# TensorE's order of work within a step of mixer B and of the hybrid layers: the projection unit first, the attention work second

## The chip, the cores and the metric

The kernel runs on one core of one Trainium2 chip. The metric is the device time of one execution in microseconds (us); the number reported is the median of the runs. Lower is better.

## What is computed

A stack of four layers on 256 tokens of width 2048, all in float32: layer A (full attention with rotary positions), a gated convolution FFN, layer B (sliding windows with three dilations), the same FFN again, and two "hybrid" layers, each with four kinds of attention side by side.

```python
h = h + mixer_a(rms_norm(h), ...)          # 16 heads
h = h + conv_ffn(rms_norm(h), ...)
h = h + mixer_b(rms_norm(h), ...)          # 24 heads of 128, three groups with dilation 1, 4, 16
h = h + conv_ffn(rms_norm(h), ...)
x = rms_norm(h, final_norm)
for l in range(2):                         # hybrid_layer
    p = split_columns(rms_norm_2(x) @ w_in + b_in)
    # stick-breaking, native sparse, forgetting and latent attention, 4 heads each, each times silu(gate)
    x = x + rms_norm_2(mix @ w_out, post_g)
```

## The kernel before

**Weights come in units.** Every weight matrix is cut into units of at most 128 x 2048 numbers (1 MB), numbered through the whole kernel. Unit u is loaded by a DMA on SyncE's queue (`load_unit`, line 218), five ahead. For full accuracy each number is split into a high part, made by ScalarE (`split_high`, line 234), and a low part, made by VectorE (`split_low`, line 242). TensorE multiplies high by high, high by low and low by high (lines 259 to 261 for products with tokens in the columns, lines 270 and 280 for products with channels in the columns). When TensorE has finished a unit it raises `w_used`, and buffers come free by that count.

**Mixer B and the hybrid layers are pipelines of steps.** Each engine has its own program: a loop over steps s, with one unit for each step (96 steps in mixer B, 82 in a hybrid layer). The first steps project the input with `w_qkv` or `w_in` (`pe_project`; 72 steps in mixer B, O0 = 66 in a hybrid layer), the last ones multiply the attention's output by the output weights (`pe_out`). The attention of a head is spread over the steps by a fixed plan: `heads_at(s, lag)` in mixer B, and `score_at`, `turn_at`, `value_at` of each `Head` in the hybrid layers. `pe_heads` does TensorE's share: values of one head, transposes of another, scores of a third. `pe_jobs` and `pe_compress` do small products and transposes that prepare keys and values, and `pe_roots` one in mixer B.

Below, U(s) is the unit of step s on TensorE and H(s) all attention work of step s (heads, jobs, compress, roots). Before, TensorE's order is ... U(s-1), H(s), U(s), H(s+1) ...

**The other engines' programs**, which the change leaves as they are, run in this order in step s of a hybrid layer (mixer B is alike):

- VectorE (`vector`): normalise the weights of the last head (`dve_weights`); evict the product of the item (a group of 2 or 4 units) that ended with U(s-1) (`dve_evict`, lines 2686 and 2690, or 2681); multiply a head's output by its gate (2766); take the scores that H(s) made (2713); low part of a head's output (2775); side work (`dve_other`); at last `split_low` of unit s+2.
- ScalarE (`scalar`): copy half of the product out of PSUM (`act_halves`, 2517); `split_high` of unit s+2; jobs; place the evicted product, with SiLU for a gate (`act_place`, 2526); copy the turned weights (2580), exponentials (2588, and 2593 to 2599 for the stick-breaking heads, the logarithm being 2596); high part of a head's output (2603).

Each of these engines does its list strictly in order, so a wait inside step s holds back what stands behind it.

**What TensorE waits for ahead of a unit**: for the high or the low part of the unit's weights; at the first unit of an item for the eviction of the item two back (`taken`; the products alternate between two pairs of PSUM banks, 4/5 and 6/7); and `pe_out` in its first step (j == 0, step O0 = 66) for the eviction of all items, the last of which ended with U(65).

In the hybrid layers units differ in length: items of type "tok" have 4 units of 258 to 512 columns, and the narrow ones are short. Steps 6 to 13, 18 to 25 and 46 to 53 have short units of about 3 us, the others take 5.5 to 5.8 us.

Of the kernel before, what the change touches and what calls it, by code (L numbers as in the profile page):

```python
# [1632 lines left out]
class MixerB:  # L1633
# [118 lines left out]
    def tensor(self, pe):  # L1752
        for s in range(B_STEPS + 24):
            self.enter.enter_pe(pe, s)
            self.pe_roots(pe, s)
            self.pe_heads(pe, s)
            if s < B_STEPS:
                self.pe_project(pe, s)
            else:
                self.pe_out(pe, s)  # L1760

    def pe_roots(self, pe, s):

        c = self.c
        if s == 5:
            self.enter.await_row(pe)
            for b in range(TB):
                ins = pe.matmul(c.bank[1][:, b:b + 1], c.row[0:1, b::2], c.ident[0:1, 0:1], start=True, stop=True)
            ins.then_inc(self.roots_made, 1)

    def pe_project(self, pe, s):
        c = self.c
        m, q = b_unit(s)
        g, kind = m % 9 // 3, m % 3
        u = self.u0 + s
        if q == 0 and m >= 2:
            pe.wait_ge(self.taken, m - 1)
        if m == 0:
            self.enter.await_chunks(pe, 8 * q + 7)
        first = 4 + 2 * (m % 2)  # L1780
        if kind < 2:
            wide_high(c, pe, u, c.psum[:, first:first + 2, :], 8 * q)
            wide_low(c, pe, u, c.psum[:, first:first + 2, :], 8 * q).then_inc(c.w_used, 1)
            return
        pe.wait_ge(c.w_low, u + 1)
        wh, wl = split_view(c, u)
        for i in range(2):
            tokens = slice(i * P, (i + 1) * P) if g == 0 else slice(i, S, 2)
            for k in range(8):
                kt = 8 * q + k  # L1790
                ins = three(pe, c.bank[first + i][:, 0:S], c.hh[:, kt, tokens], c.hl[:, kt, tokens], wh[:, k, :], wl[:, k, :],
                            kt == 0, kt == KT - 1)
        ins.then_inc(c.w_used, 1)
# [252 lines left out]
class Hybrid:  # L2046
# [235 lines left out]
    def tensor(self, pe):  # L2282
        c = self.c
        for s in range(O0 + KT):
            self.enter.enter_pe(pe, s)
            self.pe_heads(pe, s)
            self.pe_jobs(pe, s)
            self.pe_compress(pe, s)
            if s < O0:
                self.pe_project(pe, s)  # L2290
            else:
                self.pe_out(pe, s - O0)

    def pe_project(self, pe, s):
        c = self.c
# [745 lines left out]
```

## Time and profile before

| | us |
|---|---|
| median of 3 runs (3349.14 to 3351.03) | 3349.6 |
| the profiled execution | 3350.5 |
| its span, first to last instruction | 3348.7 |
| TensorE busy in that span | 3290.2 |
| VectorE busy | 2020.5 |
| ScalarE busy | 1630.5 |
| mixer B | about 1035 to 1613 in the span |
| first hybrid layer | about 2355 to 2846 |
| second hybrid layer | about 2846 to 3335 |

The span is a single execution; all rows below are of it. Times in the rows count from the start of the span. "Idle before" in square brackets is the time that the engine stood still just before the row, and the arrow tells what ended it. TensorE's matmuls are pipelined: one starts before the last has ended, so the distance between starts is the cost of one, not its printed duration.

### The profile page before, as it was taken

The numbers are of one execution on the slowest core, as the hardware profiler recorded it, in microseconds if no ns is written. First come the engines' busy times: TensorE is split into PE (matmuls) and PEld (weight loads), VectorE is DVE, ScalarE is ACT, GpSimd is POOL, SyncE is SP. The second block draws the span as 40 slices with busy tenths as digits, with TensorE's granted clock in tenths as the row PEclk, the third lists the DMA queues.
The fourth block names the chain that finished last, engine by engine and source line by source line (L and its number), as shares of the span: only waits on it lengthen the run. The fifth ranks groups of instructions, "written<-read, shape, count | busy, mean of one in ns | idle before, by whom it ended". The sixth has DMA issues, their size and how long they took to land. (4 is left out here: it accounts for less than half of the span.)

```text
span 3348.7 us, 43197 instructions
## 1 busy us (share of the span) xinstructions
PE 3290.2 (98%) x18176; PEld 2855.8 (85%) x18176; DVE 2020.5 (60%) x2448; ACT 1630.5 (49%) x1875; POOL 0.2 (0%) x4
## 2 busy tenths in 40 slices
PE   8999999999999999999999999999999999999998
PEld 7768888888888999998888888888898987898986
DVE  6765774774665555555666576576565654664654
ACT  5554553553444444443554355354454753464743
POOL 0000000000000000000000000000000000000000
PEclk9999999999999999999999999999999999999999
DMA  6525556556556555555555555555754446754544
GB/s 224 179 79 187 189 195 208 190 192 221 189 201 195 182 183 180 185 179 180 183 189 194 198 189 189 194 188 183 227 174 142 154 155 229 224 170 138 164 155 176
DMA packets 498937, 615.54 MB, mean 184 GB/s; under 512 B 21733, under 2 KB 383359, under 8 KB 497720
## 3 DMA queue, kind: packets, MB, share of 16 engines
q1 hardware_dynamic: 495288, 606.49, 54.7%
q10 hardware_dynamic: 3456, 6.29, 0.6%
q8 instruction: 144, 2.36, 0.3%
q14 instruction: 49, 0.40, 0.1%
HBM read 606.39 MB, written 12.63 MB: 185 GB/s over the span
## 5 line engine op out<-in xcount | busy, mean ns | idle before, releaser
L242 DVE TENSOR_TENSOR low<-raw,high 128x2048 fp32r<-128x2048 f32 (+3 forms) x564 | 1243.3, 2205 | 900.2 <-ACT high L234 895.5
L234 ACT ACTIVATE high<-raw 128x2048 fp32r<-128x2048 f32 (+3 forms) x564 | 1042.4, 1849 | 1259.2 <-PE bank L280 612.0
L270 PE MATMUL bank<-h,high 128*128 128x512 f32 x4672 | 1124.4, 393 | 3.0 <-PEq L1656 1.0
L270 PEld LDWEIGHTS bank<-h,high 128*128 128x128 f32 x4672 | 859.9, 188 | 178.1 <-issue 9.2
L280 PEld LDWEIGHTS bank<-h,low 128*128 128x128 f32 x4672 | 599.0, 191 | 22.7
L280 PE MATMUL bank<-h,low 128*128 128x256 f32 x4672 | 606.0, 283 | 0.0
L259 PE MATMUL bank<-high,y_high 128*128 128x512 f32 x1208 | 473.6, 392 | 4.0 <-DVE hy_tmp L2686 2.3
L261 PE MATMUL bank<-high,y_low 128*128 128x512 f32 x1208 | 471.5, 390 | 0.0
L260 PE MATMUL bank<-low,y_high 128*128 128x512 f32 x1208 | 471.4, 390 | 0.0
L259 PE MATMUL bank<-high,h 128*128 128x256 f32 (+4 forms) x1112 | 362.0, 326 | 1.9 <-PEq L1032 1.0
L261 PE MATMUL bank<-high,h 128*128 128x256 f32 (+4 forms) x1112 | 354.1, 318 | 0.0
L260 PE MATMUL bank<-low,h 128*128 128x256 f32 (+4 forms) x1112 | 353.8, 318 | 0.0
L259 PEld LDWEIGHTS bank<-high,y_high 128*128 128x128 f32 x1208 | 227.7, 188 | 51.4 <-DVE hy_tmp L2686 2.8
L261 PEld LDWEIGHTS bank<-high,y_low 128*128 128x128 f32 x1208 | 227.5, 188 | 47.8
L260 PEld LDWEIGHTS bank<-low,y_high 128*128 128x128 f32 x1208 | 227.7, 188 | 46.3
L259 PEld LDWEIGHTS bank<-high,h 128*128 128x128 f32 x1112 | 212.9, 191 | 16.8 <-issue 1.8
L260 PEld LDWEIGHTS bank<-low,h 128*128 128x128 f32 x1112 | 212.9, 191 | 13.6
L261 PEld LDWEIGHTS bank<-high,h 128*128 128x128 f32 x1112 | 212.4, 191 | 14.1
L1161 DVE SCALAR_TENSOR_TENSOR st_cv<-st_v,conv,st_cv 128x255 f32<-128x255 f32 x352 | 142.7, 480 | 0.0
L1087 ACT ACTIVATE st_cv<-st_v,conv 128x256 f32<-128x256 f32 x176 | 91.2, 591 | 4.9 <-DVE st_v L1151 4.9
L2517 ACT ACTIVATE hy_tmp<-bank 128x512 f32<-128x512 f32 x34 | 20.3, 598 | 114.7 <-PE bank L280 114.7
L2686 DVE TENSOR_TENSOR hy_tmp<-bank,hy_tmp 128x512 f32<-128x512 f32 x34 | 23.5, 692 | 80.9 <-ACT hy_tmp L2517 80.9
(263 smaller groups left out, 1884.5 us busy)
## 6 DMA issues: line engine op xcount, KB each, us to landing
raw<-in_w_up SPq DMA_DIRECT2D x176, 1024.0 KB, 5.0
raw<-in_w_down SPq DMA_DIRECT2D x88, 1024.0 KB, 5.1
raw<-in_w_in SPq DMA_DIRECT2D x84, 1024.0 KB, 5.0
raw<-in_b_w_qkv SPq DMA_DIRECT2D x72, 1024.0 KB, 4.9
raw<-in_w_out SPq DMA_DIRECT2D x32, 1024.0 KB, 5.0
raw<-in_a_w_qkv SPq DMA_DIRECT2D x24, 1024.0 KB, 5.0
raw<-in_b_w_o SPq DMA_DIRECT2D x24, 1024.0 KB, 5.0
raw<-in_a_w_o SPq DMA_DIRECT2D x16, 1024.0 KB, 5.0
```

What stands on the lines that cost most here:

```text
L234: act.activation(c.high[u % SPLIT][:, 0:n], c.raw[u % RAW][:, 0:n], ACT.Copy).then_inc(c.w_high, 1)
L242: dve.tensor_tensor(c.low[u % RAW][:, 0:n], c.raw[u % RAW][:, 0:n], c.high[u % SPLIT][:, 0:n].bitcast(F32), ALU.subtract).then_inc(c.w_low, 1)
L259: pe.matmul(out, lh, rh, start=start, stop=False, skip_group_check=skip)
L260: pe.matmul(out, lh, rl, start=False, stop=False, skip_group_check=skip)
L261: return pe.matmul(out, ll, rh, start=False, stop=stop, skip_group_check=skip)
L270: pe.matmul(banks[:, i, :], wh[:, k, i * P:(i + 1) * P], c.h[:, k0 + k, :, :].rearrange("p a n -> p (a n)"), start=k0 + k == 0, stop=False ...
L280: ins = pe.matmul(banks[:, i, 0:S], wl[:, k, i * P:(i + 1) * P], c.hh[:, k0 + k, :], start=False, stop=k0 + k == KT - 1, skip_group_check= ...
L1087: act.activation(cv[:, par, q, :], v[:, par, q, :], ACT.Identity, bias=taps[:, 3, ch:ch + 1], scale=taps[:, 1, ch:ch + 1]).then_inc(centre ...
L1161: ins = dve.scalar_tensor_tensor(out=out, in0=v[:, par, q, src], scalar=taps[:, tap, ch:ch + 1], in1=out, op0=ALU.mult, op1=ALU.add)
L2517: act.activation(self.tmp[:, n % 2, :, :], c.psum[:, bank:bank + 2, S:2 * S], ACT.Copy).then_inc(self.halved, 1)
L2686: dve.tensor_tensor(tmp, c.psum[:, bank:bank + 2, 0:S], tmp, ALU.add).then_inc(self.taken, 2)
```

## The change

In both loops the call that does the step's unit is moved ahead of the calls that do the attention work. TensorE's order becomes ... H(s-1), U(s), H(s), U(s+1) ... The boundary work of the first steps (`enter_pe`) stays at the head of the step, and the work of the other engines, their order and all semaphores stay as they are.

```diff
@@ MixerB.tensor
         for s in range(B_STEPS + 24):
             self.enter.enter_pe(pe, s)
-            self.pe_roots(pe, s)
-            self.pe_heads(pe, s)
             if s < B_STEPS:
                 self.pe_project(pe, s)
             else:
                 self.pe_out(pe, s)
+            self.pe_roots(pe, s)
+            self.pe_heads(pe, s)
@@ Hybrid.tensor
         for s in range(O0 + KT):
             self.enter.enter_pe(pe, s)
-            self.pe_heads(pe, s)
-            self.pe_jobs(pe, s)
-            self.pe_compress(pe, s)
             if s < O0:
                 self.pe_project(pe, s)
             else:
                 self.pe_out(pe, s - O0)
+            self.pe_heads(pe, s)
+            self.pe_jobs(pe, s)
+            self.pe_compress(pe, s)
```

## Rows read from the trace of the kernel before

**Rows 1.** The page, part 1: busy time, share of the span, instructions.
```profile
PE 3290.2 (98%) x18176; PEld 2855.8 (85%) x18176; DVE 2020.5 (60%) x2448; ACT 1630.5 (49%) x1875; POOL 0.2 (0%) x4
```
**Rows 2.** Waits of TensorE, whole span: us in total, times, longest.
```profile
PE bank L2419 <- ACT x L2538: 2.9, 1, 2.9
PE bank L259 <- DVE hy_tmp L2686: 2.3, 2, 1.2
...
PE bank L2372 <- ACT hy_prob_t L2580: 0.8, 2, 0.4
```
**Rows 3.** Waits of TensorE in mixer B (1036 to 1613), the whole answer.
```profile
PE bank L270 <- PEq L1032: 1.0, 1, 1.0
```
**Rows 4.** Timeline of TensorE: start, us, what; H(65), U(65), H(66), U(66).
```profile
2744.37 0.59 PE L2372 MATMUL bank<-hy_prob_t,hy_vb 128*128 128x256 f32 x2
...
2747.01 3.94 PE L270 MATMUL bank<-h,high 128*128 128x512 f32 x16
...
2752.69 0.49 PE L2356 MATMUL bank<-ident,hy_prob 128*128 128x128 f32 x3
2754.34 0.50 PE L259 MATMUL bank<-high,y_high 128*128 128x512 f32 x1 [1.15 <-DVE hy_tmp L2686]
```
**Rows 5.** Timeline of VectorE: low part of unit 67, weights, eviction in step 66.
```profile
2748.31 2.29 DVE L242 TENSOR_TENSOR low<-raw,high 128x2048 fp32r<-128x2048 f32 x1
...
2750.71 0.55 DVE L2750 TENSOR_SCALAR hy_prob<-hy_prob,hy_rec 128x128 f32<-128x128 f32 x2
2753.59 0.69 DVE L2686 TENSOR_TENSOR hy_tmp<-bank,hy_tmp 128x512 f32<-128x512 f32 x1 [2.33 <-ACT hy_tmp L2517]
```
**Rows 6.** Stretches: busy us (count) of PE, PEld, DVE, ACT, POOL; PEclk; DMA share; GB/s.
```profile
2376.20:2379.50 3.30, 3.30 (x9) 2.54 (x8) 2.29 (x1) 3.30 (x4) 0.00 (x0) 0.50 0.00 1
2338.60:2345.40 6.80, 5.06 (x16) 4.38 (x17) 2.89 (x5) 3.05 (x9) 0.00 (x0) 0.50 0.25 95
2847.20:2854.00 6.80, 3.50 (x16) 3.27 (x16) 4.02 (x10) 3.26 (x8) 0.00 (x0) 0.50 0.09 30
2752.00:2762.00 10.00, 8.85 (x47) 7.35 (x46) 4.42 (x5) 6.78 (x7) 0.00 (x0) 1.00 0.38 110
```
**Rows 7.** Timeline of TensorE: the first rows after three long waits.
```profile
2375.43 0.71 PE L535 MATMUL bank<-ident,token_stat 128*128 128x128 f32 x4 [2.19 <-ACT token_stat L520]
2340.34 0.90 PE L438 MATMUL bank<-ident,x 128*128 128x128 f32 x3 [4.36 <-DVE x L384]
2850.50 0.90 PE L438 MATMUL bank<-ident,x 128*128 128x128 f32 x3 [7.07 <-DVE x L404]
```
**Rows 8.** Timeline of TensorE: H(45), U(45), H(46), and H(49).
```profile
2639.81 0.49 PE L2356 MATMUL bank<-ident,hy_prob 128*128 128x128 f32 x3
...
2640.60 4.02 PE L270 MATMUL bank<-h,high 128*128 128x512 f32 x16
...
2646.38 0.59 PE L2372 MATMUL bank<-hy_prob_t,hy_va 128*128 128x256 f32 x2
...
2657.56 0.51 PE L2356 MATMUL bank<-ident,hy_prob 128*128 128x128 f32 x3
```
**Rows 9.** Timeline of ScalarE: copy of step 45, eviction copy and logarithm of step 46.
```profile
2641.04 0.47 ACT L2580 ACTIVATE hy_prob_t<-bank 128x384 f32<-128x384 f32 x1
...
2646.62 0.60 ACT L2517 ACTIVATE hy_tmp<-bank 128x512 f32<-128x512 f32 x1 [2.10 <-PE bank L280]
...
2651.71 0.53 ACT L2596 ACTIVATE hy_a<-hy_a 128x384 f32<-128x384 f32 x1
```
**Rows 10.** Timeline of VectorE: step 47, from the stick-breaking head to unit 49's low part.
```profile
2652.27 0.56 DVE L2725 SCALAR_TENSOR_TENSOR hy_a<-hy_prob,hy_a 128x384 f32<-128x384 f32 x1 [2.05 <-ACT hy_a L2596]
...
2655.77 1.23 DVE L242 TENSOR_TENSOR low<-raw,high 128x1032 fp32r<-128x1032 f32 x1
```
**Rows 11.** Timeline of VectorE and TensorE: low part of unit 11; H(11).
```profile
2412.70 1.25 DVE L242 TENSOR_TENSOR low<-raw,high 128x1048 fp32r<-128x1048 f32 x1 [4.81 <-ACT high L234]
...
2417.57 1.85 PE L2402 MATMUL bank<-conv,y 128*128 128x15 f32 x16
```

## The prediction

> **What bounds the kernel now.** Read the busy times first: TensorE is busy 98% of the span, VectorE 60%, ScalarE 49% [rows 1]. So TensorE's stream sets the time, and the change neither adds nor removes an instruction in it. It can pay only where TensorE stands still, and cost only where it makes it stand still. So read TensorE's waits next. Of 58 us idle (3348.7 - 3290.2) most lie at the start, the end and the boundaries between stages, which this change doesn't reach. Inside the two loops three kinds are in reach [rows 2]: one wait of 2.9 us for a ScalarE copy (L2538, step 7 of the first hybrid layer), two of 1.2 us at the first output unit (once for each hybrid layer) and two of 0.4 us for the turned weights of a head. Mixer B has no wait inside its loop at all, only 1.0 us on entering it [rows 3]. So at most about 6 us can be won. The question is what can be lost.
>
> **What the change moves.** Comparing the two orders, all H(s) move behind U(s) and nothing else changes. Among themselves the H(s) keep their distance, one unit apart. Three kinds of dependence follow.
> (a) From H to H by way of ScalarE or VectorE: same distance as before, no effect.
> (b) From a unit to attention work: one more unit of slack.
> (c) From attention work to a unit, because VectorE and ScalarE stand in their own step s waiting for H(s), with splits and evictions queued behind: one unit less. The scores (L2713) wait for H(s); behind them stand `dve_other`, the low part of unit s+2, and the eviction of step s+1. The exponentials wait for those scores; behind them stand ScalarE's eviction copy and `split_high` of step s+1.
> SyncE's loads wait for `w_used` of units alone; U(s) now ends earlier by the length of H(s), so loads start no later. Its side transfers that wait for attention work (the bias rows in mixer B, `mla_w_uq` behind `product`) are due three steps or more later; I cost them at nothing.
> For (c) the splits have two units of lead and now keep one, 5.5 to 5.8 us, or 3 us in the short steps. The only place with no lead is `pe_out` at step 66: it needs the eviction of the item that ended with U(65).
>
> **Step 66 of each hybrid layer.** Before, U(65) ends at 2752.69, three transposes (H(66)) run, TensorE waits 1.15, and U(66) starts at 2754.34: 1.65 us from unit to unit, and H(65) cost 2747.01 - 2744.37 = 2.64 earlier [rows 4]. After, H(65) comes between U(65) and U(66), and VectorE must do all of step 65 behind it before it can evict. That chain stands in the rows as it would run, counted from the start of H(65) at 2744.37: scores, low part of unit 67 (from 2748.31, 2.29 us), exponentials on ScalarE beside it, weights done at 2750.71 + 0.55 = 2751.26 [rows 5]. Before, the eviction's first half then waited for U(65) and its copy; after, U(65) is long done, and ScalarE's copy (0.6 us) follows its exponentials and fits beside the low part. So the addition takes 0.69 at once, and TensorE starts 0.06 behind it, as in the rows (2753.59 + 0.69 to 2754.34): 2752.04, which is 7.7 us from the start of H(65). H(66) now costs its own time later, 0.3. Net: 7.7 + 0.3 - 2.64 - 1.65 = 3.7 us. TensorE stands still for 7.7 - 2.64 = 5.0 us, where it was 1.15.
>
> **What a long wait does to the clock.** Around the 1.15 us wait the granted clock stayed full, 1.00, that is 2.4 GHz (2752 to 2762) [rows 6]. After waits of 2.19, 4.36 and 7.07 us [rows 7] stretches at 0.50 (1.2 GHz) follow, with 3.30, 5.06 and 3.50 us of TensorE work in them [rows 6]. Work at half clock takes twice its time, so half of it is lost: 1.65, 2.5 and 1.75 us. The wait of 5.0 lies between the last two; I take 2.1 (bounds 1.6 and 2.5). Step 66: 3.7 + 2.1 = 5.8 for each layer, 11.6 for both.
>
> **The short steps 46 to 53.** Here ScalarE is nearly full: table loads for SiLU, logarithm and exponential alternate. Before, its copy of step 45 (line 2580) starts at 2641.04 and the logarithm of step 46 ends at 2651.71 + 0.53 = 2652.24: 11.2 us, of which 2.10 were a wait for U(45), so 9.1 us of work [rows 9]. After, the transposes that the copy needs come behind U(45), whose length is 2646.38 - 2640.60 = 5.78; they end at 2639.81 + 5.78 + 0.49 = 2646.1 [rows 8], and the logarithm ends at 2655.2. VectorE's step 47 hangs on it: 2657.00 - 2652.27 = 4.7 us from there to the low part of unit 49 [rows 10], which is ready at 2659.9. TensorE would come to U(49) where H(49) started before, 2657.56 [rows 8]. A new wait of 2.3 us. In exchange ScalarE's copy no longer lags behind the turns, and the 0.4 us wait at L2372 goes. Net 1.9. The wait is nearest to the one of 2.19, so its clock loss is taken as 1.6 (bounds 0 and 1.65). Both layers: 2 x 3.5 = 7.0. At step 66 the same lag can't add up: steps 54 to 60 have almost no attention work.
>
> **Step 7 of the first hybrid layer.** The 2.9 us wait goes: the jobs of step 6 come 3 us later and ScalarE, late because of a transfer, is ready in time for those of step 7. The half clock that follows it goes too. What is late next is the weights: unit 11's low part ends at 2412.70 + 1.25 = 2413.95, behind a transfer already issued, whereas H(11) started at 2417.57 before [rows 11]; U(11) now stands at that place. So the gain is 3.6 us, not the 4 or so that the wait and its clock make up. Bounds 2.9 and 4.0.
>
> **Sum.** 11.6 + 7.0 - 3.6 = +15.0 us. Against the profiled execution: 3350.5 + 15.0 = 3365.5. That execution was 0.9 above the median, so 3364.6. Mixer B: 0, and below zero excluded, since there is no wait to remove.
>
> **Rivals.**
> (A) The clock holds through the new short wait. For: 2.3 us is hardly more than 2.19, and waits of 1.15 cost nothing. Against: the rows after 2.19. It gives 3.2 less, 3361.4.
> The Trainium skill, "TensorE: Matmul & The Clock Gate", section "Why this matters for your kernels", names a length of idle gaps between bursts of matmuls that should be avoided, and 2.3 us is under it; by that rule this rival would be right. The trace's 2.19 us wait, with half clock after it, speaks against.
> (B) The lag in the short steps is absorbed and there is no new wait. Then 2 x 0.4 are won and not 7.0 lost: 11.6 - 0.8 - 3.6 = +7.2, 3356.8. It needs ScalarE to be 2.3 us quicker than its own rows; against it.
> (C) One more place in each layer loses its lead (class c). The thinnest are the low parts at step 20, where ScalarE has a new table load for the second compressed product between exponentials, and in mixer B at step 77, behind the sums. Priced like the short steps, 2 x 3.5: 3371.6.
> (D) Not slower: the place is step 66, the mechanism that the eviction isn't held behind H(65). If the chain from H(65) to the addition took under 4.3 us (2.64 + 1.65) instead of 7.7, the step would cost nothing: +15.0 - 11.6 = +3.4, 3353.0, which is no measurable change; with (B) as well, 3345.2. Against it: VectorE works its list in order and the low part of unit 67 alone is 2.29 of the chain.
> That the change doesn't do what it says I give no chance: TensorE runs its matmuls in program order.
>
> **How the numbers follow.** Forecast 0.48, A 0.20, B 0.14, C 0.10, D 0.08. A measurement of this kernel can tell about 0.2% from no change, 6.7 us, so 3356.3 and 3342.9 are the bounds. Slower: the forecast, A, C and half of B, 0.85. Same: the rest of B and most of D, 0.12. Faster: 0.03. The range takes in A and B and just reaches C: with the clock terms and the gain at step 7 at their bounds the forecast alone spans about 3363 to 3366, B lowers it to 3356, C raises it to 3371. 3355.5 to 3371.5.
>
> **What would show each step.** In the profile after: TensorE's wait at L259 for L2686 should be 2 x 5.0 in place of 2 x 1.2, with the granted clock at 0.50 behind it; a new wait at L259 for the low part (L242) of about 2.3 in each hybrid layer, ahead of U(49); no wait at L2419 and none at L2372; none in mixer B. ScalarE's and VectorE's busy times stay the same. The forecast is wrong if VectorE's eviction at step 66 comes sooner than 7 us after H(65) begins, or if waits stand at places not named here.

## The result, and the profile after

| | before | after |
|---|---|---|
| median, us | 3349.14 (5 runs, 3348.02 to 3351.03) | 3363.55 (5 runs, 3362.2 to 3364.64) |
| span of the profiled execution, us | 3348.7 | 3360.4 |

The changed kernel is slower by 14.4 us: ratio 1.0042, 95% interval 1.0031 to 1.0053, which is 10 to 18 us. The forecast was 3364.6. The profiled pair differs by 11.7 us; the section on the forecast shows where the rest lies.

Page of after, part 1 (busy time, share of the span, instructions). Beside [rows 1] every busy time stays within 5 us and the counts are the same: TensorE does no more work, it stands still longer.

```profile
PE 3293.6 (98%) x18176; PEld 2858.4 (85%) x18176; DVE 2015.8 (60%) x2448; ACT 1625.9 (48%) x1875; POOL 0.2 (0%) x4
```

Waits of TensorE in after, whole span (us in total, times, longest). The lines for L259 answer [rows 2]: the two waits for L2686 are 4.8 where they were 1.2, two waits for a low part (L242) are new, and L2419 and L2372 no longer appear. The last line is a wait of four transposes on entering the first hybrid layer; it stood in the kernel before too (its first row is in [rows 7]) and serves below.

```profile
PE bank L259 <- DVE hy_tmp L2686: 9.7, 2, 4.8
...
PE bank L259 <- DVE low L242: 4.4, 2, 2.2
...
PE bank L535 <- ACT token_stat L520: 2.2, 1, 2.2
```

The same view of after for mixer B (1030 to 1613), the whole answer: as [rows 3], nothing inside the loop.

```profile
PE bank L270 <- PEq L1656: 1.0, 1, 1.0
PE bank L270 <- PEq L1032: 1.0, 1, 1.0
```

**Step 66 of the first hybrid layer.** Timeline of TensorE in after (start, us, what): the first row is the start of H(65), the second the last of its scores, the third U(66), the fourth U(67), to be laid beside [rows 4].

```profile
2745.91 0.59 PE L2372 MATMUL bank<-hy_prob_t,hy_vb 128*128 128x256 f32 x2
...
2747.92 0.69 PE L2389 MATMUL bank<-hy_ck,ident 4*128 4x256 f32 x2
2753.44 0.79 PE L259 MATMUL bank<-high,y_high 128*128 128x512 f32 x1 [4.83 <-DVE hy_tmp L2686]
...
2761.79 0.47 PE L259 MATMUL bank<-high,y_high 128*128 128x512 f32 x1
```

Timeline of VectorE in after: low part of unit 67, then the weights, then the addition that U(66) needs.

```profile
2749.85 2.28 DVE L242 TENSOR_TENSOR low<-raw,high 128x2048 fp32r<-128x2048 f32 x1
2752.05 0.16 DVE L2739 RECIPROCAL hy_rec<-hy_tot 128x2 f32<-128x2 f32 x1
2752.24 0.55 DVE L2750 TENSOR_SCALAR hy_prob<-hy_prob,hy_rec 128x128 f32<-128x128 f32 x2
2752.70 0.68 DVE L2686 TENSOR_TENSOR hy_tmp<-bank,hy_tmp 128x512 f32<-128x512 f32 x1
```

Timeline of ScalarE in after: the eviction copy, done 1.3 us ahead of that addition.

```profile
2750.84 0.57 ACT L2517 ACTIVATE hy_tmp<-bank 128x512 f32<-128x512 f32 x1
```

There is no idle time on VectorE in these four rows, and the bank has been complete since U(65). The addition waits for its turn in VectorE's list.

**The short steps of the first hybrid layer.** Timelines of after, ScalarE (copy of step 45, logarithm of step 46), VectorE (start of step 47, low part of unit 49) and TensorE (U(49)), beside [rows 8 to 10]:

```profile
2640.16 0.49 ACT L2580 ACTIVATE hy_prob_t<-bank 128x384 f32<-128x384 f32 x1 [2.83 <-PE bank L2356]
...
2648.58 0.53 ACT L2596 ACTIVATE hy_a<-hy_a 128x384 f32<-128x384 f32 x1
```

```profile
2649.14 0.56 DVE L2725 SCALAR_TENSOR_TENSOR hy_a<-hy_prob,hy_a 128x384 f32<-128x384 f32 x1 [2.05 <-ACT hy_a L2596]
...
2652.64 1.22 DVE L242 TENSOR_TENSOR low<-raw,high 128x1032 fp32r<-128x1032 f32 x1
```

```profile
2653.92 0.39 PE L259 MATMUL bank<-high,h 128*128 128x258 f32 x1 [2.20 <-DVE low L242]
```

From the copy to the end of the logarithm 8.95 us, from there to the end of the low part 4.75, and TensorE starts within 0.1 us of that end. ScalarE now waits 2.83 for the transposes, which come behind U(45).

**The clock.** Stretches of after (busy us and count of PE, PEld, DVE, ACT, POOL; PEclk; DMA share; GB/s). From within the wait of 4.83 the granted clock is 0.50 (1.2 GHz) for 6.83 us; behind the wait of 2.20 it is 1.00 (2.4 GHz); and on entering the second hybrid layer, from within the 7.1 us wait, which ends at 2852.47, it is 0.50 for 13.65 us.

```profile
2752.02:2758.85 6.83, 5.41 (x13) 4.25 (x14) 4.56 (x8) 3.38 (x4) 0.00 (x0) 0.50 0.01 2
2653.90:2657.30 3.40, 3.38 (x28) 3.38 (x29) 2.75 (x5) 3.37 (x5) 0.00 (x0) 1.00 0.01 2
2847.60:2861.25 13.65, 7.86 (x26) 6.59 (x27) 9.30 (x21) 8.28 (x16) 0.00 (x0) 0.50 0.17 58
```

In the kernel before the same length at the same boundary was at half clock for only half of it:

```profile
2847.17:2860.82 13.65, 9.38 (x42) 7.99 (x43) 10.84 (x21) 6.75 (x13) 0.00 (x0) 0.75 0.05 16
```

### The profile page after: what moved, and what is told of

It is laid out like the page before. It is cut to its first block and busy times, and to the rows that moved or that the text cites. A ratio compares the mean times of both kernels' runs of the same rounds, so it can differ in the third digit from the quotient of the medians.

```text
span 3360.4 us, 43197 instructions
## 1 busy us (share of the span) xinstructions
PE 3293.6 (98%) x18176; PEld 2858.4 (85%) x18176; DVE 2015.8 (60%) x2448; ACT 1625.9 (48%) x1875; POOL 0.2 (0%) x4
## 5 line engine op out<-in xcount | busy, mean ns | idle before, releaser
L242 DVE TENSOR_TENSOR low<-raw,high 128x2048 fp32r<-128x2048 f32 (+3 forms) x564 | 1241.6, 2203 | 811.8 <-ACT high L234 807.5
L259 PE MATMUL bank<-high,y_high 128*128 128x512 f32 x1208 | 475.2, 393 | 11.4 <-DVE hy_tmp L2686 9.7
L259 PE MATMUL bank<-high,h 128*128 128x256 f32 (+4 forms) x1112 | 362.6, 326 | 6.5 <-DVE low L242 4.4
L259 PEld LDWEIGHTS bank<-high,y_high 128*128 128x128 f32 x1208 | 228.5, 189 | 59.1 <-DVE hy_tmp L2686 10.5
L259 PEld LDWEIGHTS bank<-high,h 128*128 128x128 f32 x1112 | 212.8, 191 | 22.4 <-DVE low L242 5.2
L260 PEld LDWEIGHTS bank<-low,h 128*128 128x128 f32 x1112 | 213.0, 192 | 13.8
L2713 DVE CUSTOM_DVE_ANT_0 hy_prob<-bank,hy_causal 128x128 f32<-128x128 f32 x64 | 20.3, 355 | 93.0 <-PE bank L2389 93.0
L451 ACT ACTIVATE h<-bank,gain 128x256 fp32r<-128x256 f32 x96 | 37.6, 476 | 66.7 <-PE bank L438 66.3
```

Source lines behind the costliest of these rows:

```text
L242: dve.tensor_tensor(c.low[u % RAW][:, 0:n], c.raw[u % RAW][:, 0:n], c.high[u % SPLIT][:, 0:n].bitcast(F32), ALU.subtract).then_inc(c.w_low, 1)
L259: pe.matmul(out, lh, rh, start=start, stop=False, skip_group_check=skip)
L260: pe.matmul(out, lh, rl, start=False, stop=False, skip_group_check=skip)
L451: ins = act.activation(c.hh[:, kt, :], self.bank(g, k // 2)[:, k % 2 * S:(k % 2 + 1) * S], ACT.Copy, scale=c.gain[:, self.gain_col + kt:se ...
L2713: ins = dve.tensor_tensor_reduce(self.prob[:, b, at:at + nk], c.bank[0][:, at:at + nk], mask, 1.0, -3e38, ALU.add, ALU.max, self.top[:, b, ...
```

## Experiments

Theory: all of the loss lies in the hybrid layers, at two places in each (step 66, and the short steps 46 to 53), less a gain at step 7 of the first. The main rivals: part of the loss comes from elsewhere, mixer B among it; and at step 66 something other than the order on VectorE and ScalarE holds the eviction. In the diffs `unit_first` picks the new order for single steps. Differences are to the median of the kernel before in the same comparison.

### One loop at a time

`b_only` turns the order in mixer B alone, `hybrid_only` in the hybrid layers alone.

```diff
@@ b_only: MixerB.tensor
-            self.pe_roots(pe, s)
-            self.pe_heads(pe, s)
...
+            self.pe_roots(pe, s)
+            self.pe_heads(pe, s)
@@ hybrid_only: Hybrid.tensor
-            self.pe_heads(pe, s)
-            self.pe_jobs(pe, s)
-            self.pe_compress(pe, s)
...
+            self.pe_heads(pe, s)
+            self.pe_jobs(pe, s)
+            self.pe_compress(pe, s)
```

> The unit goes first in mixer B alone; the hybrid layers keep the old order. My account: mixer B has no wait to win, and its splits keep a unit of lead, so 0 us against the kernel before (within 1 us), no wait of TensorE inside mixer B. Rival (the small places of class c matter): a wait at U(77) behind the sums, 0.1 to 2 us, and the time up by as much.

> The unit goes first in both hybrid layers alone. My account: all of the change, 12 to 15 us slower than before: two waits of 4.8 us at step 66, two of 2.2 us ahead of U(49), the 2.9 us wait of step 7 gone. If mixer B had a hidden part in it, the difference would be smaller by that part. Whether half clock follows the 2.2 us waits is open: in the profile of the changed kernel it did not; the forecast said it would, 1.6 us each.

Measured: b_only 3349.4 against 3349.26, ratio 1.0000 (0.9991 to 1.0009). hybrid_only 3364.59, ratio 1.0045 (1.0031 to 1.0059). The whole change is in the hybrid layers, and in mixer B it costs nothing that can be measured, as the list of waits above says. The profiles say it more finely than the medians, which are good to about 3 us: from 230 to 2300 us, which takes in all of mixer B, TensorE loses less than 0.2 us against before in b_only and in after.

### Without the new order at step 66

`old_from_60`: the changed kernel, with the old order from step 60 of the hybrid layers on.

```diff
+            unit_first = s < 60
+            if not unit_first:
+                self.pe_heads(pe, s)
+                self.pe_jobs(pe, s)
+                self.pe_compress(pe, s)
...
-            self.pe_heads(pe, s)
...
+            if unit_first:
+                self.pe_heads(pe, s)
...
```

> The changed kernel with the old order from step 60 on in the hybrid layers (steps 54 to 60 have next to no attention work, so the switch costs nothing). My account: the chain from H(65) to the eviction is what step 66 waits for; with H(65) ahead of U(65) again the wait is back at 1.2 us and each layer wins 6 us: 11 to 12 us faster than the changed kernel, about 3351 to 3352, and full clock at step 66. Rival (ScalarE and VectorE carry their lag from the short steps to the end of the layer): the wait at step 66 stays at 3 us or more.

Measured: 3352.18 against 3349.26, ratio 1.0009 (1.0000 to 1.0018). Against +14.4 of the whole change, +2.9 is left, so step 66 costs 11.5 us in both layers together; against hybrid_only, which ran in the same comparison, it is 12.4. Waits of TensorE, 2600 to 2760, the whole answer: the wait at step 66 is 1.2 again, the one ahead of U(49) stays. (Line numbers of this kernel are 6 higher behind line 2292; L2692 is L2686.)

```profile
PE bank L259 <- DVE low L242: 2.2, 1, 2.2
PE bank L259 <- DVE hy_tmp L2692: 1.2, 1, 1.2
```

The stretch behind that same 2.2 us wait is at half clock here, unlike in after:

```profile
2655.14:2658.55 3.41, 3.11 (x14) 3.11 (x15) 2.80 (x5) 3.38 (x5) 0.00 (x0) 0.50 0.12 43
```

### Without the lag in the short steps

`old_at_45`: the changed kernel, with the old order in step 45 alone, so that ScalarE gets the transposes of that step before U(45).

```diff
+            unit_first = s != 45
...
```

> The changed kernel with the old order in step 45 alone (H(45) ahead of U(45); H(44) is empty, so nothing else moves). My account: the wait ahead of U(49) comes from ScalarE's copy of step 45, which stood behind U(45). It goes: no wait for the low part (L242) in either layer, 2 x 2.2 us less than the changed kernel, some 3359. Rival (VectorE or ScalarE are simply full in the short steps, whatever H(45) does): a wait of 1 us or more stays ahead of some unit from 47 to 53.

Measured: 3357.05 against 3349.26, ratio 1.0024 (1.0014 to 1.0033). +7.8 are left, so the short steps cost 6.6 us in both layers together (7.5 against hybrid_only). That is more than the two waits of 2.2 that I expected to win. Waits of TensorE, 2600 to 3240, the whole answer: no L242 and no L2372, while the long wait of step 66 stays.

```profile
PE bank L438 <- DVE x L404: 7.1, 1, 7.1
PE bank L259 <- DVE hy_tmp L2692: 4.8, 1, 4.8
PE bank L259 <- DVE h L462: 0.9, 1, 0.9
```

One call, in the step before the first short unit, sets whether TensorE stands still four steps later.

### One link of the chain at step 66

`low_67_later`: the changed kernel, with VectorE's low part of unit 67 moved behind the eviction.

```diff
                 self.dve_evict(dve, s, n)
+            if s == O0:
+                split_low(c, dve, self.u0 + s + AHEAD - 1)
...
-            if s < O0 + KT - 1:
+            if s < O0 + KT - 1 and s != O0 - 1:
                 split_low(c, dve, self.u0 + s + AHEAD)
```

> The changed kernel with one VectorE operation moved: the low part of unit 67 is made behind the eviction of step 66 and not ahead of it (unit 67 needs it 5 us later). My account: VectorE's list between H(65) and the eviction is the chain of 7.5 us; without those 2.2 us, weights still ahead, ScalarE's exponentials and copy come last: U(66) starts about 1.5 to 2.2 us sooner, the wait is 2.6 to 3.3 us and not 4.8, 3 to 4.5 us less in all, more if the clock stays full. Rival (ScalarE's eviction copy behind its exponentials is the bound): the wait stays near 4.8.

Measured: 3360.36 against 3349.16, ratio 1.0030 (1.0019 to 1.0041), 3.2 us less than the whole change. The wait fell from 4.83 to 3.65, less than the 2.28 of the row taken away. I expected 2.6 to 3.3 and missed the next link. Timeline of ScalarE, then of VectorE:

```profile
2751.51 0.40 ACT L2588 ACTIVATE hy_prob<-hy_prob,hy_neg 128x128 f32<-128x128 f32 x1 [5.20 <-DVE hy_neg L2718]
...
2752.70 0.58 ACT L2517 ACTIVATE hy_tmp<-bank 128x512 f32<-128x512 f32 x1
```

```profile
2752.52 0.17 DVE L2741 RECIPROCAL hy_rec<-hy_tot 128x2 f32<-128x2 f32 x1 [0.72 <-ACT hy_prob L2588]
2752.72 0.55 DVE L2752 TENSOR_SCALAR hy_prob<-hy_prob,hy_rec 128x128 f32<-128x128 f32 x2
2753.38 0.69 DVE L2688 TENSOR_TENSOR hy_tmp<-bank,hy_tmp 128x512 f32<-128x512 f32 x1
```

With the low part away, VectorE waits 0.72 for the exponentials, and two things then end together: its weights at 2753.27, and at 2753.28 ScalarE's copy, which is queued behind the same exponentials. So both engines' lists hold the eviction back. The low part was only 1.2 us of it; the rest is the round through both engines.

### Both queues cleared at step 66

`evict_early`: the changed kernel, with ScalarE's copy ahead of its step-65 exponentials, and VectorE's eviction ahead of its step-65 outputs and scores.

```diff
@@ Hybrid.scalar
-            if chan:
+            if chan and s != O0:
                 self.act_halves(act, s, n)
...
+            if s == O0 - 1:
+                self.act_halves(act, O0, len(HYBRID_ITEMS) - 1)
             self.act_heads(act, s)
@@ Hybrid.vector
-            if n is not None:
+            if n is not None and s != O0:
                 self.dve_evict(dve, s, n)
+            if s == O0 - 1:
+                self.dve_evict(dve, O0, len(HYBRID_ITEMS) - 1)
             self.dve_outputs(dve, s)
```

> The changed kernel, with the eviction that U(66) needs put ahead of H(65)'s followers in step 65: ScalarE's copy (L2517) ahead of its exponentials and VectorE's addition (L2686) ahead of the scores of step 65. My theory: the 4.83 us wait at step 66 comes only from the program order on VectorE and ScalarE, so it goes altogether (copy 0.6 and addition 0.7 from the end of U(65) fit beside H(65), 2.64 us), in both layers. The step then costs less than before, since the wait of 1.15 goes as well: 2 x 6.0 to 2 x 7.1 us less than the changed kernel, 3363.55 down to 3349 to 3352, and 1.8 us more if the longer half clock on entering the second hybrid layer hangs on the step-66 wait. The two waits of 2.2 us ahead of U(49) stay. The rival: the low part of unit 67, which is now later, or the outputs of H(65) take its place; then a wait of 2 us or more stands at U(66) or U(67) and the time stays above 3355.

Measured: 3348.64 against 3348.38, ratio 1.0001 (0.9992 to 1.0010). The loss is gone. Timelines of ScalarE, VectorE, and TensorE with the last part of H(65), then U(66) and U(67):

```profile
2747.54 0.60 ACT L2519 ACTIVATE hy_tmp<-bank 128x512 f32<-128x512 f32 x1 [1.67 <-PE bank L280]
```

```profile
2748.24 0.69 DVE L2690 TENSOR_TENSOR hy_tmp<-bank,hy_tmp 128x512 f32<-128x512 f32 x1 [2.65 <-ACT hy_tmp L2519]
```

```profile
2749.35 0.69 PE L2389 MATMUL bank<-hy_ck,ident 4*128 4x256 f32 x2
2749.97 0.50 PE L259 MATMUL bank<-high,y_high 128*128 128x512 f32 x1
...
2755.81 0.47 PE L259 MATMUL bank<-high,y_high 128*128 128x512 f32 x1
```

The copy starts on the end of U(65), the addition 0.7 later, beside H(65), and U(66) starts without any idle time. So the wait is a matter of program order on the two other engines alone. The two waits ahead of U(49) are still there; the gain at step 7 pays for them. The same work from U(66) to U(67) takes 5.84 us here (2749.97 to 2755.81) and 8.35 in after (2753.44 to 2761.79): 2.5 us is what the half clock behind the 4.83 us wait costs.

### The gain at step 7

`entry_only`, `entry_and_short` and `only_step_7` are the kernel before with the new order in steps 0 to 8, in steps 0 to 8 and 46 to 53, and in step 7.

```diff
+            unit_first = s < 9                   # entry_only
+            unit_first = s < 9 or 46 <= s < 54   # entry_and_short
+            unit_first = s == 7                  # only_step_7
```

> The kernel before with the unit first in steps 0 to 8 of the hybrid layers alone. My account: the gain of 3.6 us at step 7 of the first hybrid layer without any of the losses: 3345.5, no wait at L2419. Rival (the gain is given back at the next transfer, because the loads and not the jobs set the pace there): less than 2 us gained, and a wait at L259 in steps 8 to 12.

> As entry_only, and the unit first in steps 46 to 53 too, with the old order in step 45 and from 54 on. My account: 3.6 us at step 7, and the two waits of 0.4 us (0.5 with what stands around them) for the turned weights go with no new one, since ScalarE's copy of step 45 is early: 3344.5. Rival (the short steps are full either way): the 0.4 us waits go and a wait for a low part of 0.5 us or more comes in their place, 3345.5 or more.

> The kernel before with the unit first in step 7 of the hybrid layers alone. My theory of the gain at the entry: TensorE loses 3.5 us in step 7 of the first hybrid layer because it stands before a job whose buffer ScalarE clears late, and U(7) ahead of that job is enough to cover it. Then the 2.9 us wait at L2419 is gone and the time is that of the kernel with steps 0 to 8 turned, about 3345.7 us (0.999 of the kernel before). The rival: it needs the whole entry turned, since ScalarE stands late because earlier jobs come late; then a wait of 1 us or more stays at L2419 and the gain is 2 us or less.

Measured: entry_only 3345.7 against 3349.16, ratio 0.9988 (0.9979 to 0.9996); entry_and_short 3346.04, ratio 0.9988 (0.9979 to 0.9997); only_step_7 3345.17 against 3348.38, ratio 0.9988 (0.9979 to 0.9997). All three gain about 3.3 us. With the new order in steps 46 to 53, and not in 45, the waits at L2372 vanish from the list and no new one above 0.2 us comes, but the time doesn't show it.

In only_step_7 both theories were half right: the time came out as mine says, but the wait didn't go, as the rival has it. Timelines of ScalarE and TensorE:

```profile
2397.93 1.08 ACT L234 ACTIVATE high<-raw 128x1048 fp32r<-128x1048 f32 x1 [5.41 <-DMA raw<-in_w_in]
2398.92 0.58 ACT L2544 ACTIVATE x<-bank 128x512 f32<-128x512 f32 x1
```

```profile
2399.55 0.66 PE L2425 MATMUL bank<-ident,hy_stage 128*128 128x128 f32 x4 [1.38 <-ACT x L2544]
```

ScalarE stands before a transfer for 5.4 us, with the copy that TensorE's job needs queued behind. With U(7) ahead of the job, 1.4 of the 2.9 us remain. The clock goes the same way: the kernel before ran at half clock behind its 2.9 us wait, and here it stays full. So a gain doesn't need the wait to go away, only to become short. How the 3.2 us divide is not shown: between this profile and that of before, step 7 differs by 2.4 us only, and b_only, whose hybrid layers are those of before, had a wait of 2.5 and full clock in its profile and lost 1.7 us less there than before did. What one execution loses at step 7 varies by that much.

### A version that beats both

`best`: the kernel before, with the new order in steps 0 to 8, 46 to 53 and from 60 on in the hybrid layers, and the early eviction of evict_early.

```diff
+            unit_first = s < 9 or 46 <= s < 54 or s >= 60
...
```

> The kernel before with the unit first in steps 0 to 8, 46 to 53 and from 60 on in the hybrid layers, with the early eviction of the run evict_early. It should have none of the waits at L2419, L2372, L2686 and L242: 3345.9 us (steps 0 to 8 and 46 to 53 turned) less two waits of 1.15 at step 66: 3343.5, 0.9983 of the kernel before, faster than both kernels. The rival: the early eviction moves the wait to another place at step 66, then 3346 or more.

Measured: 3342.07 against 3348.38, ratio 0.9979 (0.9971 to 0.9988): 6.3 us faster than before and, by the two ratios, 21 us faster than the changed kernel. The waits at L2419, L2372, L2686 and L242 are all gone. What the order wins or loses thus depends on where it is used, and on the other engines' lists being turned with it.

It also overturned a guess. On entering the second hybrid layer the clock of before was at half for 6.83 us, and of after for 13.65. In after, hybrid_only, old_at_45 and low_67_later, all with a long wait at step 66, it was 13.65 each time, so I took the one for the cause of the other. But best has no such wait and shows the same:

```profile
2837.64:2851.29 13.65, 8.32 (x27) 6.95 (x28) 9.76 (x21) 7.82 (x16) 0.00 (x0) 0.50 0.15 54
```

## Why the forecast was right, point by point

"By equal work" below means that the start of one and the same matmul is compared in two profiles, here just behind each of the places.

**Busy engines don't matter, waits do; mixer B costs nothing.** Shown by the page, the waits and b_only. The waits of after also settle rivals B and C in that execution: the new wait is there, and none stands at another place.

**Step 66.** Forecast 5.8 for each layer; old_from_60 gives 11.5 / 2 = 5.75. The parts: idle time 5.0 forecast and 4.83 found; from the start of H(65) to U(66) 7.7 forecast and 7.53 found (2745.91 to 2753.44), because the addition starts before the printed end of the weights. The half clock behind it was sized 2.1 and measured 2.5. By equal work in the profiled pair the step cost 6.0 and 6.1. That the 5.75 sits so close to 5.8 is luck (against hybrid_only it is 6.2, and each comparison is good to some 3 us); the waits and the 6.0 are the better evidence. The sign of being wrong, an eviction sooner than 7 us after H(65) begins, holds for its end only: it begins 6.8 us after and ends 7.5 us after, where the working had 6.9 and 7.6. Rival D named what had to be true for no loss: a chain under 4.3 us. evict_early is that case made on purpose. The chain was not one list, though: my working let the exponentials and ScalarE's copy run beside the low part, which is right, but it hid that they would hold TensorE for 3.65 us without it (low_67_later).

**Short steps.** The new wait was forecast at 2.3 and is 2.20; ScalarE's stretch 9.1 and 8.95; VectorE's 4.7 and 4.75. By equal work TensorE lost 1.8 in each layer without the clock, forecast 1.9. The clock term was 1.6 for each wait. That was the step I sized worst: in after the clock held behind both. Rival A was right in this execution. In the five kernels with this wait unchanged there are ten such waits, and half clock follows three: two in old_from_60, one in low_67_later. Where it follows it costs 1.4: from U(49) to U(50) takes 4.6 us in old_from_60, at half clock, and 3.2 in evict_early. So 3 x 1.4 / 10 = 0.4 for each wait would have been a better term than 1.6, and the forecast of both layers 4.6, not 7.0. The 6.6 that old_at_45 shows leans to the higher, but since old_at_45 has no waits at L2372, the short steps cost 0.8 less against the kernel before, 5.8, and each of the two comparisons is uncertain by 3 us or more; it doesn't decide between 4.6 and 7.0. Counted with the bound of 0 that the clock term has there, the forecast alone would reach down to 3360 and not 3363; the stated range holds that too.

The Trainium skill, "TensorE: Matmul & The Clock Gate", section "Why this matters for your kernels", asks for no idle gaps over about 3 us between bursts. The runs here agree in the main: half clock followed every wait of 3.65 us and more, and seven of ten waits of 2.2 were free. But the other three were not, and the 2.2 us wait at L535 was followed by it in ten of the twelve profiles, a 1.7 us wait at 208 us in eight.

**Step 7.** Forecast 3.6; 3.5 by entry_only, 3.6 by equal work in the profiled pair. The limit that the forecast named, unit 11's low part, is real but loose: TensorE waits for it at U(11) for 0.5 us in evict_early, 0.3 in hybrid_only, 0.2 in old_at_45, and not in after. By equal work the gain against the profile of before lies between 2.0 (hybrid_only) and 4.4 (entry_only), so the exact 3.6 is partly luck.

**The sum.** Step 66 11.5, short steps 6.6 - 0.8 and step 7 -3.5 make 13.8, measured 14.4, forecast 15.0. With 0.4 for the clock term of the short steps the forecast would have been 12.6, so that the total came within 0.6 owes something to luck. The profiled pair goes another way to its 11.7: in after 2.2 are won before step 7 is reached, most of it because a half clock at 208 us of before is missing; then -3.6, +1.8, +6.0, +1.8 for the longer half clock at the boundary, +1.8 and +6.1. The first of these is chance: at 208 us nothing of the change has run, and of the twelve profiles four lack that half clock. The +1.8 is a term that the forecast lacks, and its cause stays open. Over the twelve profiles that stretch is 6.83 in five (before, old_from_60, entry_only, only_step_7, evict_early), 10.24 in two (b_only, entry_and_short) and 13.65 in five. Every kernel with a long wait at step 66 is among the last, and best, without one, too. It may be chance altogether. No run tells the two apart.

## What to carry to other kernels

When one engine's work is reordered inside a step, list for each result what stands behind its consumer on the consumer's engine: here TensorE's own stream was as good in either order, and the loss came from an eviction standing behind work that now ended later. If such an order is turned, turn the consumer's list with it; undone step by step, the change held a gain of 3 us and, with two calls moved on the other engines, a version 6 us faster than before. A short wait should be priced as its length plus a chance of the clock's loss, not plus the whole loss.

## What the hardware showed that was not expected

- The granted clock behind one and the same wait differs between executions. Behind 2.2 us ahead of U(49) it was half in three cases of ten; behind the 2.2 us at L535 in ten of twelve (not in hybrid_only and only_step_7, where the work behind it took 1.6 us less); behind a wait of 1.7 us at 208 us, in mixer A (in before one of 0.75 stands 3 us ahead of it), in eight of twelve; behind 2.9 at L2419 in before, and not behind 2.5 in b_only. Waits of 1.4 us and less in the hybrid layers (1.38 in only_step_7, 1.15 at step 66 of before) left it full. Waits of 3.65 and 4.83 were followed by half clock each time, eight of eight.
- Its length differs as well: 3.41 or 6.83 us behind the waits of step 66, and 6.83 to 13.65 behind the 7.1 us wait at the boundary. One such stretch moves a profiled execution by 1.4 to 2.1 us, so single profiles that differ by 2 or 3 us say little of a kernel.
